# A diagonal state-space layer in a four-layer trunk: from a scan over 256 steps to a scan over 64 chunks of four steps

## The reference

```python
    dt = jnp.exp(log_dt.astype(f32))[:, None]
    mag = jnp.exp(lam_re * dt)
    ang = lam_im * dt
    a_re, a_im = mag * jnp.cos(ang), mag * jnp.sin(ang)
...
    bb_re = f_re[..., None] * b_re - f_im[..., None] * b_im
    bb_im = f_re[..., None] * b_im + f_im[..., None] * b_re
    u = h.reshape(bsz, l, S5_GROUPS, S5_GROUP).astype(f32)
    bu_re = jnp.einsum('blgc,gpc->lbgp', u, bb_re)
    bu_im = jnp.einsum('blgc,gpc->lbgp', u, bb_im)
...
    _, _, x_re, x_im = lax.associative_scan(_complex_affine_combine, (a_re_t, a_im_t, bu_re, bu_im), axis=0)
    y = (jnp.einsum('lbgp,gcp->blgc', x_re, c_re.astype(f32))
         - jnp.einsum('lbgp,gcp->blgc', x_im, c_im.astype(f32)))
    y = y.reshape(bsz, l, D_MODEL) + d_skip.astype(f32) * h.astype(f32)
    y = jax.nn.gelu(y).astype(h.dtype)
    val, gate = jnp.split(y @ w_glu, 2, axis=-1)
    return val * jax.nn.sigmoid(gate)
```

## Time and profile before

| | us |
|---|---|
| median of 3 runs | 2088.29 (2087.94 to 2091.82) |
| the profiled execution | 2090.42, its span 2088.8 |
| TensorE busy | 1861.2 (89%) |
| VectorE, ScalarE, GpSimd busy | 1329.5, 1006.8, 404.0 |
| dense feed-forward 0, end on TensorE | about 362 |
| scale of norm 2 | 419.5 |
| first matmul of the GLU | 610.8 |
| norm 3 | from about 658 |

### The profile page before, as it was taken

How to read it: one execution, slowest core, us unless ns; L and a number is a source line. 1 busy time by engine, 2 the same in 40 slices (tenths; PEclk the granted TensorE clock), 3 DMA queues, 4 the chain that set the end, 5 groups by cost and what they waited for, 6 DMA issues and landing times.

```text
span 2088.8 us, 26100 instructions
## 1 busy us (share of the span) xinstructions
PE 1861.2 (89%) x10454; PEld 1642.7 (79%) x10454; DVE 1329.5 (64%) x1148; ACT 1006.8 (48%) x865; POOL 404.0 (19%) x433
## 2 busy tenths in 40 slices
PE   6989999067778999999998989999998899999997
PEld 6979998033347898888887789999887688888886
DVE  4425554068854688888885644443542688888886
ACT  4454333021114576666664433333445566666664
POOL 5328999834420000000000000000001000000000
PEclk9999999578789899999999989999999899999998
DMA  8614655312234699999996403544550499999993
GB/s 288 207 32 164 210 182 180 91 48 76 76 123 132 225 321 321 319 322 330 323 319 207 148 24 131 181 163 160 172 202 31 135 323 329 329 321 319 321 321 138
DMA packets 248275, 430.42 MB, mean 206 GB/s; under 512 B 6504, under 2 KB 210320, under 8 KB 248192
## 3 DMA queue, kind: packets, MB, share of 16 engines
q1 hardware_dynamic: 243520, 414.64, 57.7%
q0 software_dynamic: 4672, 14.60, 2.2%
HBM read 419.77 MB, written 9.44 MB: 205 GB/s over the span
## 4 chain that ended last, share of the span: by engine, by line
PE 72%; POOL 12%; DVE 10%; ACT 3%; issue 2%; DMA 1%; DVEq 0%; POOLq 0%; SPq 0%; ACTq 0%
PE PS L271 19%; PE PS L273 19%; PE PS L272 19%; PE PS L1016 4%; DVE wlo L310 3%; DVE uu L1106 2%; POOL tg L933 2%; PE PS L1253 1%; POOL tg L936 1%; POOL tm L934 1%; POOL tm L935 1%; POOL tm L931 1%; DVE vvv L1125 1%; PE PS L1298 1%; POOL tm L932 1%
## 5 line engine op out<-in xcount | busy, mean ns | idle before, releaser
L310 DVE TENSOR_TENSOR wlo<-raw,whi 128x3072 fp32r<-128x3072 f32 (+3 forms) x279 | 870.4, 3127 | 346.8 <-ACT whi L303 345.8
L303 ACT ACTIVATE whi<-raw 128x3072 fp32r<-128x3072 f32 (+3 forms) x279 | 708.4, 2540 | 421.7 <-PE PS L273 420.0
L271 PE MATMUL PS<-wlo,hT_hi 128*128 128x384 f32 (+3 forms) x1936 | 635.0, 328 | 15.5 <-DVE hT_lo L1505 3.4
L273 PE MATMUL PS<-whi,hT_hi 128*128 128x384 f32 (+3 forms) x1936 | 628.6, 325 | 0.0
L272 PE MATMUL PS<-whi,hT_lo 128*128 128x384 f32 (+3 forms) x1936 | 628.4, 325 | 0.0
L271 PEld LDWEIGHTS PS<-wlo,hT_hi 128*128 128x128 f32 x1936 | 368.3, 190 | 28.2 <-DVE wlo L310 6.9
L272 PEld LDWEIGHTS PS<-whi,hT_lo 128*128 128x128 f32 x1936 | 368.5, 190 | 3.7 <-issue 0.7
L273 PEld LDWEIGHTS PS<-whi,hT_hi 128*128 128x128 f32 x1936 | 368.1, 190 | 0.3
L423 POOL TENSOR_TENSOR stat<-stat,cst 128x1 f32<-128x1 f32 x18 | 14.9, 832 | 815.7 <-DVE stat L400 809.6
L271 PE MATMUL PS<-wlo,mhi 128*128 128x512 f32 x352 | 143.3, 407 | 16.4 <-DVE mlo L1518 16.4
L272 PE MATMUL PS<-whi,mlo 128*128 128x512 f32 x352 | 139.1, 395 | 0.0
(11 more groups left out here) (306 smaller groups left out, 2425.9 us busy)
## 6 DMA issues: line engine op xcount, KB each, us to landing
raw<-in_moe_w_gate_up SPq DMA_DIRECT2D x96, 1536.0 KB, 7.2
raw<-in_moe_w_down SPq DMA_DIRECT2D x48, 1536.0 KB, 7.1
raw<-in_ffn_w_gate_up SPq DMA_DIRECT2D x28, 1536.0 KB, 6.9
raw<-in_moe_w_gate_up SPq DMA_DIRECT2D x32, 1024.0 KB, 6.2
raw<-in_ffn_w_down SPq DMA_DIRECT2D x14, 1536.0 KB, 6.4
raw<-in_sb_w_qkv SPq DMA_DIRECT2D x12, 1536.0 KB, 7.5
raw<-in_moe_w_down SPq DMA_DIRECT2D x16, 1024.0 KB, 6.3
s_tables<-tg POOLq DMA_DIRECT2D x16, 512.0 KB, 3.8
```

The costliest lines, as they stand in the source:

```text
L271: pe.matmul(o, sh, mlw, start=start, stop=False, skip_group_check=True)
L273: return pe.matmul(o, sh, mh, start=False, stop=stop, skip_group_check=True)
L303: act.activation(whi[p0 % SPL][:, 0:n], raw[p0 % RAW][:, 0:n], ACT.Copy).then_inc(hi_done, 1)
L310: dve.tensor_tensor(wlo[p0 % SPL][:, 0:n], raw[p0 % RAW][:, 0:n], whi[p0 % SPL][:, 0:n].bitcast(F32), ALU.subtract).then_inc(lo_done, 1)
```

## The change

The recurrence is taken over 64 chunks of four steps. With j, i for steps in a chunk, d for a distance, the state at a chunk's end is a^4 times that of the chunk before plus four taps a^(3-j) B u_j; these taps are matmuls (32 channels by 128 states, 64 chunks; `inputs`). VectorE rotates and scans these 64 chunk states with a^4 for four tiles at once, with a table `decay` that holds |a|^4 and is zero where a new tile begins. An output is the sum of three parts: the state ahead of the chunk times C a^(i+1) (`outputs`, then copied out and turned back by matmuls in `joined`), the influence inside the chunk by four short kernels K_d = C a^d B (`kernels`, `within`), and the skip d_skip as a diagonal matrix. The main loop has 8 steps (of 128 channels) where it had 32.

All constants of one step form one table of 128 x 3072 floats: G (C times powers 0 to 4 of a), B, W (B times f and its powers, by channel) and R (rotation). GpSimd computes B, W and R during the dense feed-forward, VectorE computes G there, one step's table in each of the eight steps. Both parts are written to DRAM and read through the weight ring as eight pieces of 1.5 MB between the third and the fourth piece of the layer's weights. B and C are laid out on the host, a transposition without arithmetic. GpSimd's part of the main loop and the transposes of B and C on TensorE are gone. The GLU may begin with the first 128 channels.

The core of the diff:

```diff
-        tabs = nc.dram_tensor("s5_tables", [ST, P, 2 * L], F32, kind="Internal").ap()
+        tabs = nc.dram_tensor("s5_tables", [KC, P, SLOT], F32, kind="Internal").ap()
+        afd = nc.dram_tensor("s5_rows_af", [ST, 8, P], F32, kind="Internal").ap()
...
         def load_piece(sp, p0, src=None, de=0):
-            if p0 >= RAW:
+            if TAB0 <= p0 < base["moe0"]:
+                sp.wait_ge(s5_o, p0 + 1 - TAB0 + KC - RAW)
+            elif p0 >= RAW:
                 sp.wait_ge(lo_done, p0 - RAW + 1 + MOE_PIECES * de)
...
...
+                if f == 0 and j < JD:
+                    s5_powers_dve(dve, j)
                 if 2 <= j < JD:
                     split_lo(dve, b0 + ND["d", j - 2] + SPL)
                 if j < JD:
...
         def s5_tables_pool(pool):
+            pool.dma_start(ff["g_nat"][:].rearrange("p k r q o -> p k (r q o)"),
+                           s5_bc[:, :, 512:768].rearrange("k p n -> p k n")).then_inc(s5_cn, 16)
+            def load(c):
+                pool.dma_start(nat[:], s5_bc[c, :, 0:512]).then_inc(s5_nat, 16)
+                for r in range(4):
+                    src = afd[4 * c + r:4 * c + r + 1].rearrange("a q s -> a (q s)")
+                    pool.dma_start(af[32 * r:32 * r + 32].rearrange("p n q s -> p (n q s)"),
+                                   src.to_broadcast([32, 8 * P])).then_inc(s5_afr, 16)
+            load(0)
...
+            for c in range(KC):
+                if c >= 1:
+                    pool.wait_ge(s5_tw, 16 * c)
...
+                product(o_r[:, 0], o_r[:, 1], ca, sa, cb, sb_, t4, ALU.subtract, ALU.add)
+                pool.wait_ge(s5_nat, 16 * (c + 2))
...
+                product(o_b[:, :, 0], o_b[:, :, 1], fr, fi, bs4[:, :, 0], bs4[:, :, 1], t3, ALU.add, ALU.subtract)
+                pool.wait_ge(s5_afr, 64 * (c + 1))
...
+                product(o_w[:, :, 0], o_w[:, :, 1], af[:, :, 0], af[:, :, 1], b0, b1, tw, ALU.add, ALU.subtract)
+                pool.dma_start(tabs[c, :, 1280:3072], out[:]).then_inc(s5_tw, 16)
+                if c + 1 < KC:
+                    load(c + 1)
+                pool.wait_ge(s5_gd, c + 1)
+                pool.dma_start(tabs[c, :, T_G], ff["g_out"][:].rearrange("p r q i o -> p (r q i o)")).then_inc(s5_gw, 16)
+            pool.wait_ge(s5_tw, 16 * KC)
+            pool.memset(decay[:, :, 0:1], 0.0)
+            pool.memset(s5m["kb"][:], 0.0)
+            pool.memset(s5m["xx"][:], 0.0)
+            pool.wait_ge(s5_gw, 16 * KC)
+            pool.tensor_copy(decay[:, :, 1:], mag.rearrange("p (t a) -> p t a", a=1).to_broadcast([P, ST, L // 4 - 1]))\
+                .then_inc(s5_zero, 1)
+
+        def s5_powers_dve(dve, c):
+            if c == 0:
+                dve.wait_ge(s5_cn, 16)
+                dve.wait_ge(s5_pa, 1)
+            else:
+                dve.wait_ge(s5_gw, 16 * c)
+            dve.tensor_copy(o[:, :, :, 0, :], cn_[:, c])
+            dve.tensor_tensor(o[:, :, 0, 1:5, :], cr, pr, ALU.mult)
+            link(dve.tensor_tensor(tmp[:], ci, pi, ALU.mult))
+            dve.tensor_tensor(o[:, :, 1, 1:5, :], cr, pi, ALU.mult)
+            link(dve.tensor_tensor(o[:, :, 0, 1:5, :], o[:, :, 0, 1:5, :], tmp[:], ALU.subtract))
+            link(dve.tensor_tensor(tmp[:], ci, pr, ALU.mult))
+            dve.tensor_tensor(o[:, :, 1, 1:5, :], o[:, :, 1, 1:5, :], tmp[:], ALU.add).then_inc(s5_gd, 1)
...
+            def inputs(c):
+                for q in range(2):
+                    for j in range(4):
+                        for r in range(4):
+                            v = slice(32 * r, 32 * r + 32)
+                            last = pe.matmul(PS[:, r, 64 * q:64 * q + 64], w[v, 3 - j, q, :], u[v, :, j],
+                                             start=(j == 0), stop=(j == 3), skip_group_check=True)
+            def kernels(c):
+                for q in range(2):
+                    for r in range(4):
+                        last = pe.matmul(PS[32 * r:32 * r + 32, 6, 0:P], b[:, r, q, :],
+                                         g[:, r, q, 0:4, :].rearrange("p i o -> p (i o)"), start=(q == 0), stop=(q == 1),
+                                         skip_group_check=True)
+            def within(c):
+                pe.matmul(o, s5m["dd"][:, c % 2, :], u, start=True, stop=False, skip_group_check=True)
+                for d in range(4):
+                    last = pe.matmul(by4(o)[:, :, d:4], kb[:, c % 2, d, :], by4(u)[:, :, 0:4 - d], start=False,
+                                     stop=False, skip_group_check=True)
+            def outputs(c):
+                for r in range(4):
+                    for q in range(2):
+                        last = pe.matmul(o[:, :, 32 * r:32 * r + 32], xx[:, c % 2, q, r, :], g[:, r, q, 1:5, :],
+                                         start=(q == 0), stop=(q == 1), skip_group_check=True)
+            def joined(c):
+                for i in range(4):
+                    last = pe.matmul(o[:, :, i], y1[0:64, c % 2, i * P:(i + 1) * P], ident[0:64, 0:64], start=False,
+                                     stop=(i == 3), skip_group_check=True)
+            for i in range(KC + 2):
+                if i < KC:
+                    inputs(i)
+                if i >= 2:
+                    joined(i - 2)
+                if i < KC:
+                    kernels(i)
+                if 1 <= i <= KC:
+                    within(i - 1)
+                    outputs(i - 1)
...
         def s5_loads(sp):
+            for c in range(KC):
+                sp.wait_ge(s5_tw, 16 * (c + 1))
+                sp.wait_ge(s5_gw, 16 * (c + 1))
+                if c < RAW:
+                    sp.wait_ge(lo_done, base["s5"] + c)
+                else:
+                    sp.wait_ge(s5_o, c - RAW + 1)
+                sp.dma_start(table(c)[:], tabs[c]).then_inc(raw_in[(TAB0 + c) % RAW], 16)
```

More of the change, by code:

```diff
@@ L68, in constants, with lay_out_s5 @@
     return c
+def lay_out_s5(b_re, b_im, c_re, c_im, d):
+    by_channel = np.zeros((KC, 4, 2, SG, 2, 2, SS), np.float32)
+    by_state = np.zeros((2, KC, 2, SS, 4, 2, 2, SG), np.float32)
+    for q, (b, c) in enumerate(((b_re, c_re), (b_im, c_im))):
+        b, c = b.reshape(KC, 4, 2, SS, SG), c.reshape(KC, 4, 2, SG, SS)
+        for g in range(2):
+            by_channel[:, :, g, :, q, g, :] = b[:, :, g].transpose(0, 1, 3, 2)
+            by_state[0, :, g, :, :, q, g, :] = b[:, :, g].transpose(0, 2, 1, 3)
+            by_state[1, :, g, :, :, q, g, :] = c[:, :, g].transpose(0, 3, 1, 2)
+    parts = [by_channel.reshape(KC, P, 256), by_state[0].reshape(KC, P, 256), by_state[1].reshape(KC, P, 256)]
+    return np.ascontiguousarray(np.concatenate(parts, axis=2)), np.ascontiguousarray(d.reshape(KC, P).T)
 def widths(total, w=W):
@@ L281, in at, with table, table_in @@
             return pair[0][ix], pair[1][ix]
+        TAB0 = base["s5"] + RAW - 1
+        assert KC % RAW == 0
+        def table(c):
+            return raw[(TAB0 + c) % RAW]
+        def table_in(eng, c):
+            eng.wait_ge(raw_in[(TAB0 + c) % RAW], 16 * ((TAB0 + c) // RAW + 1))
         def psize(p0):
@@ new lines, in s5_tables_pool @@
+            glink(pool, pool.tensor_tensor(power(3, 0), a_, b_, ALU.subtract))
+            pool.tensor_tensor(a_, power(2, 0), power(1, 1), ALU.mult)
+            glink(pool, pool.tensor_tensor(b_, power(2, 1), power(1, 0), ALU.mult))
+            pool.tensor_tensor(power(3, 1), a_, b_, ALU.add).then_inc(s5_pa, 1)
+            pool.wait_ge(s5_pa, 1)
+            square(s5_par[:, 1, :], s5_par[:, 2, :], wc, ws)
+            square(wc, ws, wc, ws)
+            glink(pool, pool.tensor_tensor(mag, mag, mag, ALU.mult))
@@ L1035, in s5_pe @@
                         for k in range(KC):
+                            if i == 0 and q == 0 and t == 0:
+                                pe.wait_ge(s5_yl, k + 1)
                             last = split3(pe, PS[:, 4 * (i % 2) + 2 * q + t, 0:w],
@@ new lines, in s5_act @@
+            act.wait_ge(s5_nat, 16 * (KC + 1))
+            act.wait_ge(s5_zero, 1)
+            for i in range(KC + 2):
+                if i >= 2:
+                    k = i - 2
+                    act.wait_ge(s5_ac, k + 1)
+                    if k >= 2:
+                        act.wait_ge(s5_yl, k - 1)
+                    act.activation(s5m["yt"][:, k % 2, :], PS[:, 5 + 2 * (k % 2), 0:L], ACT.Gelu_apprx_tanh)\
+                        .then_inc(s5_ge, 1)
+                    act.wait_ge(s5_ge, k + 1)
+                    act.activation(hT_hi[:, k, :], s5m["yt"][:, k % 2, :], ACT.Copy).then_inc(s5_yh, 1)
+                if i < KC:
+                    if i >= 2:
+                        act.wait_ge(s5_cv, i - 1)
+                    act.activation(s5m["dd"][:, i % 2, :], ident, ACT.Copy, scale=dT[:, i:i + 1]).then_inc(s5_dd, 1)
+                    act.wait_ge(s5_k, i + 1)
+                    for r in range(4):
+                        v = slice(32 * r, 32 * r + 32)
```

(13 more changed lines are left out.)

414 lines of the change are left out of this document (174 added, 240 removed).

## The result

The changed kernel takes 2007.96 us (2007.2 to 2010.3, four runs) against 2088.7 (2087.94 to 2091.82): a ratio of 0.9614, interval 0.9599 to 0.9629, that is 81 us or 3.9% less. The forecast was 2040, with a range from 2005 to 2092. The profiled execution took 2010.3 us with a span of 2008.7 (2090.42 and 2088.8 before).

The account below looks back on a forecast made before the run. The layer's 249 us were taken as GpSimd waiting, then VectorE pacing. The norm 43.5 us later but the GLU at 563, not 610.8, gave 2090.4 - 48 = 2042 profiled; the median, 2.1 lower, gave 2040, range 2005 to 2092.

Parts of the forecast that it names:

- What bounds the kernel: State-space layer before the change: 249 us, some 55 with all waiting for GpSimd and 191 with VectorE as pacer.
- the direction: Whole kernel: faster by over 0.2% (4 us) at a chance of 0.84, slower 0.12, within 0.04.
- GpSimd's own work: Tables in the dense feed-forward: prelude 32 us as before, products 14.1 us a chunk, issues 4.1, landing 6 from the issue.
- What the change adds in the dense stage: Dense feed-forward: VectorE waits for G's write-out, step 1's gate product at 247 not 201, norm at 463, 43.5 us later.
- the part with the largest price: Dense feed-forward: VectorE waits for the previous G's write-out, queued behind GpSimd's tables; 46 us of delay at step 1 alone.
- GpSimd paces: Dense steps: GpSimd's period of 33.3 us exceeds TensorE's own 25.7; bounds 27 and 40 us.
- The rivals on the period, 40 or 27 us: GpSimd's table period in the dense stage: 40 us gives 2080, chance 8%; 27 us gives 2003, chance 13%.
- What it removes in the layer: Norm's scale to GLU: 7 us, eight chunks of 10.5 paced by TensorE, a 9 us tail; GLU at 563, not 610.8.
- The page against the taps: Layer's taps: the skill's 107 ns per weight load would make 64 loads 6.8 us a chunk, not 3.1; kernel at 2070.
- Serial taps: Layer's taps: four row groups don't overlap at 64 columns, 3.7 us more a chunk, 2070; chance 12%.
- cold clock: Layer: small matmuls leave TensorE's clock at 1.2 GHz, 18.4 us a chunk, 63 us more, 2103; chance 12%.
- prompt tables: GpSimd's tables in the dense stage: period 27 us, 37 us less, 2003; chance 13%.

## Why the prediction was right or wrong

**What bounds the kernel, and the direction: right.** The layer gives back far more than the dense stage pays, 119 against 42 us. The forecast had the signs and the dense part nearly to the microsecond.

**GpSimd's own work: right.** Chunks from 214.8 (216), table 0 issued at 229.73 (230), its eighteen products 14.6 us (14.1). In the fourth chunk the splits cost 9.2 us (9.3) and G 2.3 (3.9). The landing, for which I had 6 us, was 6.6 on average (4.6 to 9.2). Three full meetings with splits came only in the third to fifth chunk, where the products took 26.1 to 26.4 us (27.0 forecast); in the others it was 20.9 to 24.1, so two small errors of opposite sign are in the period. The Trainium skill, "SBUF — State Buffer", section "Who interferes with whom", says that a VectorE instruction with two inputs in SBUF contends with a GpSimd instruction that reads SBUF, and that the lock on the ports which they share is exclusive. The trace agrees: a product that met a split of 3.3 us took 4.26 to 4.41 us, not 1.26.

**What the change adds in the dense stage: right in every time.** First wait over at 239.25 (240), the second gate product at 246.14 (247), period 32.6 on average (33.3), last gate product 441.8 (445), x updated at 456.4 (457 to 459), the norm's scale at 461.9 (463), with GpSimd last by 1.74 us (2). What I called "the part with the largest price", the wait of VectorE for G, is only where the price shows: in the run with two G buffers the first wait is gone, most of it comes back one step on and ahead of the norm, and the time is the same within the intervals. The price is GpSimd's queue of eight tables, as "GpSimd paces" had said, and the runs that shorten this queue show it with 21, 52 and 56 us. The rivals on the period, 40 or 27 us, did not come.

**What it removes in the layer: right in mechanism, wrong in size.** From the third chunk on TensorE paces and VectorE is next, idle 1.2 to 3.4 us (mostly 1.75) ahead of its first product. The norm to the first taps took 7.0 us (7). But I took 10.5 us for a chunk, and it is 7.4: eight times 3.1 are 25 of the 32 us that the forecast was too high. The measured chunk lies outside the 9.2 to 12 us on which most of my chance stood, and the measured time outside 2018 to 2062. By the terms:

- the clock: I raised 9.2 to 10.5, and it was 1.00 in most of the layer: 1.3 us;
- taps: 3.1 foreseen, 2.05 measured. The bound from the old taps' weight loads, 0.048 us a record, was one for 256 columns; 64 columns cost less;
- kernels 1.2 and 0.58; changes of shape 0.7 and no gap to be seen (what they may cost inside a part's own time cannot be told apart);
- against it, joined 0.8 and 1.03; within, with the skip, 1.6 and 1.84 (I had counted 832 columns; they are 256 of the skip and 640, and my own 0.43 us for 256 would have given 1.5); outputs 1.75 and 1.89.

The last chunk's tail was 5.7 us by the same count (533.78 less 468.87, less eight chunks of 7.4), not 9, and the norm began 1.1 us early. With 1.6 in the GLU and 1.5 behind, neither of which I had counted, that is 32 us: 2042 forecast for the profiled execution, 2010.3 measured.

**The page against the taps: right in direction for another order, too high in size.** The Trainium skill, "TensorE: Matmul & The Clock Gate", says in "Part 3: Packing small matmuls — row/col tiling" that weight loads overlap with matmuls in flight only where the row group differs. The runs agree: 0.032 us a record with four groups in turn, 0.044 with two, 0.077 with one. The cost by columns that I had cited from its section on LDWEIGHTS would be 6.8 us for the 64 records; in a row, at full clock, they took 4.94, so here the measurement decides against 107 ns a load (only the second chunk's taps, largely at the lower clock, took longer, 8.44).

**The rivals.** "Serial taps" and "cold clock" named real mechanisms that this kernel's order of taps largely avoids (but for two cold stretches of some 3 us each). I had priced them apart and given each its own chance. The run with the taps in a row shows that they come together, and cost 44.5 us, less than the 63 of the cold clock alone, since the clock falls only for part of each chunk. The direction was no luck. But the measured 2008 lies where I had put the prompt tables (2003), by chance and for another reason: those would have come from a period of 27 us, and it was 32.6.

## What to carry to other kernels

When a wait appears in the trace of an in-order engine, ask what queue ends it before pricing the wait: a second buffer took 40 us of idle time from its place, most of it came back further on, and the end moved by less than the intervals can tell, while six products moved to the engine that had stood waiting for them gave 52 us. Here these products, which GpSimd made beside VectorE's work, were cheaper on VectorE once GpSimd was done. For small row-tiled matmuls let the row group be the innermost loop; the order alone was worth 44 us here.

## What was unexpected of the hardware

- The granted clock fell from 1.00 to 0.50 once for each of the last six blocks of 32-row matmuls that ran on one row group at a time, five times for some 6.8 us and once for 3.4, though TensorE had no idle time in or behind the block. With two groups in turn it fell behind four of the last six blocks for about 3 us, with four behind one of six. The cause is open.
- Records of 64 columns on 32 rows cost 0.032, 0.044 and 0.077 us each with four, two and one row groups in turn.
- Matmuls of 32 rows by 128 columns, 64 by 128, 128 by 32, 128 by 128 and 128 by 64 follow one another within a chunk of 7.39 us with no gap in the records at the changes. Whether a change costs time inside a part's own records is not shown.
